# Gated linear attention: decays, products and transposes of the next step beside the scores and outputs of this one

## The reference

```
def gla_chunked(q, k, v, logg, s0):
    '''S_t = diag(alpha_t) S_{t-1} + k_t^T v_t, o_t = q_t S_t (chunked form).'''
    ...
    bcum = jnp.cumsum(logg.reshape(Bsz, n, C, H, DK), axis=2)
    ...
    o_intra = jnp.einsum('bnhij,bnjhv->bnihv', attn, vc)
    btot = bcum[:, :, -1]
    ds = jnp.einsum('bnjhd,bnjhv->bnhdv', kc * jnp.exp(btot[:, :, None] - bcum), vc)
    ...
        return dec[..., None] * s + d, s
    ...
    o_inter = jnp.einsum('bnihd,bnhdv->bnihv', qc * jnp.exp(bcum), jnp.moveaxis(s_prev, 0, 1))
    o = (o_intra + o_inter).reshape(Bsz, L, H, DV)
```

## Time and profile before

| | |
|---|---|
| runs, us | 2723.35, 2724.76, 2725.25; median 2724.76 |
| profiled execution, us | 2720.09; its span 2718.3 |
| mean granted TensorE clock over the span | 0.926 of 2.4 GHz |
| PE busy | 2398.0 us, 88% |
| DVE, ACT, POOL busy | 903.1, 504.7, 95.5 us |
| GLA scan, layer 0 and 1, us from the span's start | 471.18 to 579.13 and 1816.06 to 1924.00 |

### The profile page before, as it was taken

The page is one execution under the profiler, slowest core; times in us unless marked ns, Lnnn a source line. Parts: engine busy times, 40 slices in busy tenths (PEclk is TensorE's granted clock), DMA queues, the critical chain, the costliest instruction groups (busy, mean ns, idle before and its releaser), DMA issues. The chain is left out here.

```text
span 2718.3 us, 36041 instructions
## 1 busy us (share of the span) xinstructions
PE 2398.0 (88%) x15000; PEld 1484.4 (55%) x15000; DVE 903.1 (33%) x1552; ACT 504.7 (19%) x924; POOL 95.5 (4%) x64
## 2 busy tenths in 40 slices
PE   6999999879989988987479999997899899889873
PEld 3546754654567555554245466545545675555542
DVE  2246512441468323110212553124415682321102
ACT  2133302220133112000020332022101330211000
POOL 0000000000012000000000000001000210000000
PEclk8999999889989988998789999998999899799986
DMA  7231052103411214999552211321134012169993
GB/s 247 90 114 63 1 185 93 63 32 124 155 47 47 86 44 191 402 419 421 223 193 89 92 62 61 129 105 47 49 135 152 21 47 93 37 270 413 420 419 111
DMA packets 142423, 407.07 MB, mean 150 GB/s; under 512 B 9447, under 2 KB 34535, under 8 KB 133545
## 3 DMA queue, kind: packets, MB, share of 16 engines
q1 hardware_dynamic: 128744, 388.37, 37.7%
q10 hardware_dynamic: 11776, 9.97, 1.1%
q0 software_dynamic: 1728, 6.29, 0.7%
HBM read 388.59 MB, written 16.02 MB: 149 GB/s over the span
## 5 line engine op out<-in xcount | busy, mean ns | idle before, releaser
L297 PE MATMUL ps<-hT,ring 128*128 128x384 f32 x1344 | 460.1, 503 | 26.7 <-ACT hT L418 12.1
L297 PEld LDWEIGHTS ps<-hT,ring 128*128 128x128 f32 x1344 | 261.7, 197 | 212.0 <-issue 39.5
L297 PE MATMUL ps<-ring,hT 128*128 128x512 f32 x768 | 335.8, 598 | 3.8 <-PEq L1198 3.8
L297 PE MATMUL ps<-arena,ring 128*128 128x384 f32 x768 | 253.0, 492 | 11.4 <-DVE arena L480 7.4
L297 PEld LDWEIGHTS ps<-ring,hT 128*128 128x128 f32 x768 | 146.9, 192 | 191.9 <-issue 190.8
L297 PEld LDWEIGHTS ps<-arena,ring 128*128 128x128 f32 x768 | 146.9, 192 | 115.7 <-issue 17.4
L1686 PE MATMUL ps<-ring,arena 128*32 128x256 f32 x2432 | 146.9, 404 | 30.9 <-DMA ring<-in_e_w 26.4
L1686 PE MATMUL ps<-arena 128*32 128x256 f32 x2432 | 145.2, 401 | 25.9 <-DMA arena<-in_e_w 25.9
L329 PE MATMUL ps<-cst,arena 128*128 128x128 f32 x472 | 85.4, 336 | 92.9 <-DVE arena L1962 33.6
L329 PEld LDWEIGHTS ps<-cst,arena 128*128 128x128 f32 x472 | 67.9, 173 | 123.0 <-DVE arena L1962 36.1
L1686 PEld LDWEIGHTS ps<-ring,arena 128*32 128x32 f32 x2432 | 87.1, 116 | 87.2 <-issue 40.1
(11 more groups left out here) (283 smaller groups left out, 2673.1 us busy)
## 6 DMA issues: line engine op xcount, KB each, us to landing
ring<-in_e_w SPq DMA_DIRECT2D x48, 2048.0 KB, 15.9
arena<-in_e_w SPq DMA_DIRECT2D x48, 2048.0 KB, 17.9
ring<-in_w_in SPq DMA_DIRECT2D x36, 2048.0 KB, 8.4
ring<-in_w_ada SPq DMA_DIRECT2D x24, 2048.0 KB, 8.1
ring<-in_a_wo SPq DMA_DIRECT2D x4, 2048.0 KB, 11.8
ring<-in_b_wo SPq DMA_DIRECT2D x4, 2048.0 KB, 8.3
ring<-in_c_wo SPq DMA_DIRECT2D x4, 2048.0 KB, 8.7
ring<-in_w_out SPq DMA_DIRECT2D x4, 2048.0 KB, 7.9
```

Source lines behind the costliest of these rows:

```text
L297: ins = pe.matmul(out, a, b, start=(i == 0), stop=(i == len(pairs) - 1))
```

## The change

The steps are staggered. Ahead of the loop each engine does the first part of step 0: prefix sums, decays, products, transposes and their copies. Inside the loop each does that part for step s+1 while it does scores, mask, outputs and state of step s: TensorE has the prefix sums of s+1 before the scores of s, then a gate tile, the transposes of s+1, and only then the state products and outputs of s. VectorE clamps s+1 before the mask of s and does products and key copy of s+1 before it evacuates s. So the loop does gate tiles 1 to 6, and one, in place of two, is left behind it.

Buffers are doubled or reused for it: `kt`, `qtT` and `ktT` have two halves, taken by the step's parity. Exp of minus the clamped sums goes straight into `kt`, and the key product is done in place. Exp of the sums goes into the step's slice of `logdec`, which nothing reads any more by then, and the query product is done there in place. The one-column copy and its semaphore are gone: ScalarE waits for the clamp's own. Some waits of an engine for its own last instruction are left out. The DMAs are the same, in the same order.

```diff
@@ -123,7 +123,7 @@
         names = (
             "xin", "cond_clear", "cond_ready", "params_in", "cache_in", "squares_ready", "root_ready", "weighted",
             "h_ready", "cqn_ready", "ckvn_ready", "sq_ready", "summed", "stat_ready", "head_root", "rotary_in",
-            "nmax_ready", "abs_ready", "soft_ready", "logdecay_ready", "clamped_ready", "decay_ready",
+            "nmax_ready", "abs_ready", "soft_ready", "logdecay_ready", "decay_ready",
             "qk_ready", "gla_state_in", "scaled_state", "state_ready", "o_ready", "conv_ready",
             "xbc_ready", "ssd_state_in", "diff_ready", "decayed_ready", "mask_ready", "xw_ready",
             "yoff_ready", "y_ready", "merged_ready", "chosen_ready", "iota_in", "sums_ready", "cleared", "starts_ready", "picked", "tokens_in", "hidden_ready", "moe_ready", "stored",
@@ -986,12 +986,9 @@
             gla_s = carve(9216, 2, H_B, DV)
             gla_p = carve(11264, 2, H_B, DV)
             clamped = carve(13312, 512)
-            up = carve(13824, H_B * DK)
-            down = carve(14336, H_B * DK)
-            qt = carve(20992, H_B, DK)
-            kt = carve(21504, H_B, DK)
-            qtT = carve(22016, H_B, P)
-            ktT = carve(22528, H_B, P)
+            kt = carve(20992, 2, H_B, DK)
+            qtT = carve(22016, 2, H_B, P)
+            ktT = carve(13824, 2, H_B, P)
             att = carve(23040, H_B, P)
             ecol = carve(23552, 2, H_B, 2)
             stat_b = carve(23568, NT * H_B)
@@ -1009,29 +1006,45 @@
                     for i in range(2):
                         token_major(pe, W_OG + i, ("og", i))
                     pe.wait_ge(*following(pe, "logdecay_ready"))
-                    for s, (d, t) in enumerate(SCAN):
+
+                    def front(s):
+
+                        d, t = SCAN[s]
                         pe.matmul(claim(pe, ("b", s)), rel(d), logdec[:, d, t, :], start=True, stop=True).then_inc(*makes(("b", s)))
                         out = claim(pe, ("ec", s))
                         for h in range(H_B):
                             ins = pe.matmul(out[:, 2 * h:2 * h + 2], logdec[:, d, t, DK * h:DK * h + DK],
                                             cst[:, C_SEL:C_SEL + 2], start=True, stop=True)
                         ins.then_inc(*makes(("ec", s)))
-                        gate_pe(pe, W_GB, "gb", s)
+
+                    def turn(s):
+
+                        d, t = SCAN[s]
                         pe.wait_ge(*following(pe, "qk_ready"))
-                        transposed(pe, ("qtT", s), [qt[:, h, :] for h in range(H_B)])
-                        transposed(pe, ("ktT", s), [kt[:, h, :] for h in range(H_B)])
+                        transposed(pe, ("qtT", s), [logdec[:, d, t, DK * h:DK * h + DK] for h in range(H_B)])
+                        transposed(pe, ("ktT", s), [kt[:, s % 2, h, :] for h in range(H_B)])
+
+                    front(0)
+                    gate_pe(pe, W_GB, "gb", 0)
+                    turn(0)
+                    for s, (d, t) in enumerate(SCAN):
+                        if s + 1 < len(SCAN):
+                            front(s + 1)
                         pe.wait_ge(*read(("qtT", s)))
                         pe.wait_ge(*read(("ktT", s)))
                         out = claim(pe, ("att", s))
                         for h in range(H_B):
-                            ins = pe.matmul(out[:, P * h:P * h + P], ktT[:, h, :], qtT[:, h, :], start=True, stop=True)
+                            ins = pe.matmul(out[:, P * h:P * h + P], ktT[:, s % 2, h, :], qtT[:, s % 2, h, :], start=True, stop=True)
                         ins.then_inc(*makes(("att", s)))
+                        gate_pe(pe, W_GB, "gb", s + 1)
+                        if s + 1 < len(SCAN):
+                            turn(s + 1)
                         if s not in LAST:
                             for g in range(2):
                                 out = claim(pe, ("ds", s, g))
                                 for h in (2 * g, 2 * g + 1):
                                     c = DV * (h % 2)
-                                    ins = pe.matmul(out[:, c:c + DV], kt[:, h, :], v_b[:, t, h, :], start=True, stop=True)
+                                    ins = pe.matmul(out[:, c:c + DV], kt[:, s % 2, h, :], v_b[:, t, h, :], start=True, stop=True)
                                 ins.then_inc(*makes(("ds", s, g)))
                         pe.wait_ge(*read(("att", s)))
                         if t:
@@ -1042,10 +1055,10 @@
                                 c = DV * (h % 2)
                                 pairs = [(att[:, h, :], v_b[:, t, h, :])]
                                 if t:
-                                    pairs.append((qtT[:, h, :], gla_s[:, d, h, :]))
+                                    pairs.append((qtT[:, s % 2, h, :], gla_s[:, d, h, :]))
                                 ins = matmuls(pe, out[:, c:c + DV], pairs)
                             ins.then_inc(*makes(("o", s, g)))
-                    for g in range(len(SCAN), KD):
+                    for g in range(len(SCAN) + 1, KD):
                         gate_pe(pe, W_GB, "gb", g)
 
                 @block.scalar
@@ -1061,25 +1074,38 @@
                             s = bank((("og", i), t))
                             act.activation(og[:, t, 512 * i:512 * i + 512], s, ACT.Silu).then_inc(*reads((("og", i), t)))
                             act.wait_ge(*read((("og", i), t)))
-                    for s in range(len(SCAN)):
-                        act.wait_ge(*following(act, "clamped_ready"))
-                        act.activation(up, clamped, ACT.Exp).then_inc(*counts("act_step"))
-                        act.wait_ge(*counted("act_step"))
-                        act.activation(down, clamped, ACT.Exp, scale=-1.0).then_inc(*counts("decay_ready"))
+
+                    def exps(s):
+
+                        d, t = SCAN[s]
+                        act.wait_ge(*read(("b", s)))
+                        act.activation(kt[:, s % 2, :, :].rearrange("p h d -> p (h d)"), clamped, ACT.Exp, scale=-1.0
+                                       ).then_inc(*counts("act_step"))
                         act.wait_ge(*made(("ec", s)))
+                        act.activation(logdec[:, d, t, :], clamped, ACT.Exp).then_inc(*counts("decay_ready"))
                         act.activation(ecol[:, s % 2, :, :],
                                        bank(("ec", s))[:, 0:2 * H_B].rearrange("p (h e) -> p h e", e=2),
                                        ACT.Exp).then_inc(*reads(("ec", s)))
-                        act.wait_ge(*read(("ec", s)))
-                        gate_tile_act(act, "gb", gT_b, s)
+
+                    def queries_turned(s):
+
                         act.wait_ge(*made(("qtT", s)))
-                        act.activation(qtT, quad(bank(("qtT", s))), ACT.Copy).then_inc(*reads(("qtT", s)))
-                        act.wait_ge(*read(("qtT", s)))
+                        act.activation(qtT[:, s % 2, :, :], quad(bank(("qtT", s))), ACT.Copy).then_inc(*reads(("qtT", s)))
+
+                    exps(0)
+                    gate_tile_act(act, "gb", gT_b, 0)
+                    queries_turned(0)
+                    for s in range(len(SCAN)):
+                        if s + 1 < len(SCAN):
+                            exps(s + 1)
+                        gate_tile_act(act, "gb", gT_b, s + 1)
+                        if s + 1 < len(SCAN):
+                            queries_turned(s + 1)
                     act.wait_ge(*following(act, "o_ready"))
                     act.activation(sq_b, o_b.rearrange("p t (h d) -> p (t h) d", d=DV), ACT.Square).then_inc(*counts("sq_ready"))
                     act.wait_ge(*following(act, "stat_ready"))
                     act.activation(stat_b, stat_b, ACT.Sqrt).then_inc(*counts("head_root"))
-                    for g in range(len(SCAN), KD):
+                    for g in range(len(SCAN) + 1, KD):
                         gate_tile_act(act, "gb", gT_b, g)
 
                 @block.gpsimd
@@ -1112,23 +1138,38 @@
                     dve.scalar_tensor_tensor(out=logdec, in0=soft, scalar=-1.0 / GATE_NORM, in1=logdec,
                                              op0=ALU.mult, op1=ALU.add).then_inc(*counts("logdecay_ready"))
                     dve.wait_ge(*counted("logdecay_ready"))
-                    for s, (d, t) in enumerate(SCAN):
+
+                    def clamp(s):
+
                         dve.wait_ge(*made(("b", s)))
                         dve.tensor_scalar(clamped, bank(("b", s)), CLAMP, -CLAMP, ALU.min, ALU.max).then_inc(*reads(("b", s)))
-                        dve.wait_ge(*read(("b", s)))
-                        dve.tensor_copy(stat_b[:, 0:1], cst[:, 0:1]).then_inc(*counts("clamped_ready"))
+
+                    def queries_keys(s):
+
+                        d, t = SCAN[s]
                         dve.wait_ge(*following(dve, "decay_ready"))
```

(25 more changed lines are left out.)

## The result

The changed kernel takes 2678.86 us (median of four runs, 2675.81 to 2683.17) against 2724.06 for the kernel before (also of four, one more than were known for the forecast): a ratio of 0.9838, with a 95% interval of 0.9825 to 0.985. The forecast was 2693 with a range from 2684 to 2704.

A forecast was written before the change was run, and what follows sets the result against it. Bound: a chain through all engines, TensorE covered only by the gate tile. Steps sum to 90.35 us plus 1.7 for clock, 92.05 per layer; 31.8 saved in both gives 2688.3, or 2693 at the median's level; range 2684 to 2704.

The forecast's parts named there:

- the chain of a step: Previous outputs' end to the transposes: forecast 8.88 us before steps 2 and 3, 10.33 before steps 4 and 5.
- What is removed: Forecast's savings: one-column copy, 0.19 us per chain; waits of 0.90 to 1.67 before scores and 0.85 for the mask.
- signs that it named for being wrong: Waits over 3 us before transposes, clock at 0.50 for more than 7 us in a scan, or a grown tail.
- The single wait before the scores of step 0: TensorE waiting for the query copy in the one step without cover: 0.15 us.
- one stretch of 1.7 us at half clock: Clock loss behind the two 2.43 us waits of the scan: 1.7 us per layer, ends 0 and 10.4.
- Rival (a): Clock stays down after the long waits: 10.4 in place of 1.7 us a layer, 2710 us; chance 0.10.
- rival (c): Clock at half speed behind waits before the transposes in every step: 3.3 us per layer lost, 2731 us; chance 0.03.
- The tail and the idle time in it: After the last outputs: tail keeps its 15.57 us, TensorE's idle time grows from 5.09 to about 10.3 us.
- The gate tile: TensorE's filler work in a step, taken at 5.25 us; a seventh stands before the last outputs.
- The key product stayed at GpSimd's mercy: VectorE's key product, running beside GpSimd's state scaling, was forecast to stay lengthened at 2.27 us.
- rival (b): GpSimd no longer catches the key product, 2683 us, or the clock never falls, without its 1.7 us 2679; chance 0.07.

The follow-up runs named there:

- b1: Changed kernel with ScalarE's waits for its own half-sum Exp and query copy put back, holding both table loads: 2696.02 us, ratio 0.9902.
- a1: Changed kernel with ScalarE waiting for its own query copy again, holding only the Exp's table load: 2696.74 us, ratio 0.9893.
- a4: Changed kernel run again with no edit: 2682.49 us, ratio 0.9844.
- b2: Changed kernel with GpSimd's state scaling made to wait for the key product: 2679.34 us, ratio 0.9834.
- b3: Changed kernel with GpSimd's scaling behind the key product and gate tile 6 behind the last outputs: 2666.93 us, ratio 0.9798.
- b4: Changed kernel with the later GpSimd scaling, no gate tile in the loop's first step and three tiles behind the loop: 2669.71 us, ratio 0.9802.

## Why the prediction was wrong

**The step that failed** is the chain of a step in "What is removed": it took only the one-column copy out ("0.19 less per chain") and carried the rest over from the earlier trace rows as a whole, with 1.28 us of table load between clamp and Exp. That waits of an engine for itself were left out was known from the diff, and the sum has no term for it. Their cost was not in the waiting. With two waits ahead of an Exp, the clamp's stood in front of the table load; with one, nothing did, and the load ran in ScalarE's idle time.

The runs put numbers on it. With the load held (b1) the stretch is 104.3 and 107.5 us, 105.9 in the mean against 106.5 forecast, so order, covers and clock were worked out right for the kernel that I had in mind. The load alone is 4.8 us in layer 0 and 8.1 in layer 1 (a1, clock included), 12.8 in both, and 14.2 by the totals of a1 and a4. Of the 45 us gained the forecast had 31.8, 13 too few. None of the signs that it named for being wrong appeared (waits over 3 us, a clock at 0.50 for more than 7 us, a longer tail): all of them looked for a kernel slower than forecast.

**The waits.** Forecast 0.98, 0.98, 2.43 and 2.43 before the transposes; held, they are 0.84, 0.84, 2.29 and 2.29; in the changed kernel 0, 0, 0.95 and 0.95. The single wait before the scores of step 0 (0.15) is gone too, since the Sigmoid's load is ahead; held in b1, it costs the 0.2 us.

**The clock.** I took one stretch of 1.7 us at half clock for every second of the long waits. With the waits as forecast (a1, b1) there was none in layer 0 and one behind each in layer 1, 3.3 us for two: right in the mean of the layers, and in neither of them. In the changed kernel no wait is over 0.95 us and the clock held, which is 1.7 us a layer of the miss, and a consequence of the first step. Rival (a) and rival (c), with the rule of the Trainium skill cited there (TensorE: Matmul & The Clock Gate, "A second HAM failure mode: psum-queue depth-cycling"), did not come about: two short waits a layer left the clock at 1.00.

**Smaller terms.** The tail and the idle time in it were right to 0.1 us. The gate tile was taken at 5.25 us; with the scores in front of it, it takes 5.16 (0.5 us for six of them). VectorE's products and ScalarE's Exps start 0.53 to 0.61 us apart, without a wait of the engine for itself between them, instead of 0.66 to 0.73. The key product stayed at GpSimd's mercy as forecast (2.38 us against 2.27), so rival (b) named the measured time by luck, for the wrong reason. Its 2679 came from a product of 0.69 us, which only the kernels with the later scaling have (b2, b3 and b4).

**The range** had a bound for each price that was seen as unknown, and none for a term that was carried over as measured. The chain's table load had its row, with the releaser written beside it: that it waited for VectorE at all, when it reads nothing that VectorE writes (the changed kernel runs it 8 us ahead of the clamp), was the thing to see.

## What to carry to other kernels

Look at a table load that has a releaser: it could run in idle time, and what bound it here was a wait that the code sets for another instruction. An engine's waits for its own last instruction weren't free here even though they never waited, because with them another wait was set in front of the load. Two such lines were worth 21 us of the stretches (15 of the totals) in the old order and 13 of the stretches in the new. When work is staggered, end the pipeline by hand: the filler that covers a wait inside the loop stood in the way of the last step, and behind that step it was worth 8 us more in both layers together.

## What was unexpected of the hardware

The same wait of 2.29 us in the same place of the program left the clock at full twice in layer 0 and took it to half twice in layer 1, in a1 as in b1: 104.11 against 107.38 us, and 104.31 against 107.54. Whether the clock falls is thus not a matter of a wait's length alone, and a single fall more or less moves a total by about 1.7 us. What decides it, no run here shows.

A VectorE product with two inputs in SBUF took 2.38 us beside GpSimd's scaling and 0.68 without it, and the scaling itself took 1.90 us on its own instead of 2.41: here it is one line of waiting that keeps the two apart.

```profile
524.42 1.90 POOL L1122 TENSOR_TENSOR arena<-arena 128x1024 f32<-128x1024 f32 x1 [13.40 <-DVE arena L1155]
```
